# Scattering expert outputs with a bare one-hot selection, split rows, and token weights applied in the residual sum

## The reference

```python
def moe_ffn(h, w_router, w_e_gate, w_e_up, w_e_down):
    logits = jnp.einsum('bsd,de->bse', h, w_router, preferred_element_type=jnp.float32)
    top_vals, top_idx = lax.top_k(logits, TOP_K)          # TOP_K = 2
    top_w = jax.nn.softmax(top_vals, axis=-1)
    combine = jnp.sum(jax.nn.one_hot(top_idx, N_EXPERTS) * top_w[..., None], axis=-2)
    y = jnp.zeros_like(h)
    for e in range(N_EXPERTS):                            # 8 experts, inner width 1408
        y = y + combine[..., e:e + 1] * swiglu(h, w_e_gate[e], w_e_up[e], w_e_down[e])
    return y
...
x = x + moe_ffn(h, w_router[i], w_exp_gate[i], w_exp_up[i], w_exp_down[i])
```

## Time and profile before

| | |
|---|---|
| median of 3 runs | 1165.09 us (1164.87 to 1167.19) |
| profiled execution | 1167.5 us, its span 1165.8 us |
| PE busy | 1100.5 us (94%) |
| PEld busy | 942.7 us (81%) |
| DVE busy | 823.7 us (71%) |
| ACT busy | 669.9 us (57%) |
| expert stage | about 728 us to 1160 us of the span |

### The profile page before, as it was taken

The page is one execution under the profiler, slowest core; times in us unless marked ns, Lnnn a source line. Parts: engine busy times, 40 slices in busy tenths (PEclk is TensorE's granted clock), DMA queues, the critical chain, the costliest instruction groups (busy, mean ns, idle before and its releaser), DMA issues.

```text
span 1165.8 us, 16875 instructions
## 1 busy us (share of the span) xinstructions
PE 1100.5 (94%) x6535; PEld 942.7 (81%) x6535; DVE 823.7 (71%) x1110; ACT 669.9 (57%) x956; POOL 73.9 (6%) x119
## 2 busy tenths in 40 slices
PE   4999999988999998999999996999999999999997
PEld 3979777778999997979787775888888888788885
DVE  3577766875545545457866776689898888989885
ACT  3567655454434435457755553576767676677763
POOL 4001430000000000000521000000000000000000
PEclk9999999998999999999999996799999999999999
DMA  5553354465446444345344454499899898999992
GB/s 180 202 181 118 116 174 145 145 215 202 161 170 239 153 163 151 101 145 181 102 161 144 147 193 166 142 322 339 301 324 365 290 346 307 381 305 349 342 327 90
DMA packets 147670, 250.19 MB, mean 215 GB/s; under 512 B 5166, under 2 KB 108676, under 8 KB 147588
## 3 DMA queue, kind: packets, MB, share of 16 engines
q1 hardware_dynamic: 145808, 246.89, 61.6%
q10 hardware_dynamic: 1780, 2.19, 0.6%
HBM read 248.02 MB, written 1.05 MB: 214 GB/s over the span
## 4 chain that ended last, share of the span: by engine, by line
PE 82%; DVE 10%; ACT 4%; issue 2%; POOL 1%; DMA 1%; ACTq 0%; DVEq 0%; POOLq 0%
PE PS L622 26%; PE PS L1077 9%; PE PS L1078 9%; PE PS L1079 9%; PE PS L938 5%; PE PS L940 5%; PE PS L939 5%; DVE w_lo L402 4%; PE PS L1048 2%; PE PS L710 2%; DVE m_lo L1759 2%; PE PS L648 1%; PE PS L1036 1%; ACT w_hi L393 1%; PE PS L805 1%
## 5 line engine op out<-in xcount | busy, mean ns | idle before, releaser
L402 DVE TENSOR_TENSOR w_lo<-ring,w_hi 128x1536 fp32r<-128x1536 f32 (+1 forms) x192 | 311.6, 1633 | 126.4 <-ACT w_hi L393 125.9
L393 ACT ACTIVATE w_hi<-ring 128x1536 fp32r<-128x1536 f32 (+1 forms) x192 | 264.8, 1388 | 152.5 <-PE PS L940 85.8
L1759 DVE TENSOR_TENSOR m_lo<-ring,m_hi 128x512 fp32r<-128x512 f32 (+2 forms) x256 | 185.7, 754 | 91.9 <-ACT m_hi L1275 90.2
L1275 ACT ACTIVATE m_hi<-ring 128x512 fp32r<-128x512 f32 (+2 forms) x256 | 157.5, 631 | 141.7 <-PE PS L622 139.1
L1077 PE MATMUL PS<-w_hi,hTe 128*96 128x384 f32 (+1 forms) x384 | 131.5, 342 | 0.7 <-issue 0.7
L622 PE MATMUL PS<-m_hi,h_hi 128*128 128x512 f32 (+2 forms) x352 | 125.2, 356 | 2.1 <-DVE m_lo L1759 2.1
L1078 PE MATMUL PS<-w_hi,hTe 128*96 128x384 f32 (+1 forms) x384 | 124.5, 324 | 0.0
L1079 PE MATMUL PS<-w_lo,hTe 128*96 128x384 f32 (+1 forms) x384 | 124.5, 324 | 0.0
L622 PE MATMUL PS<-m_lo,h_hi 128*128 128x512 f32 (+2 forms) x352 | 120.5, 342 | 0.0
L622 PE MATMUL PS<-m_hi,h_lo 128*128 128x512 f32 (+2 forms) x352 | 120.5, 342 | 0.0
L938 PE MATMUL PS<-h_hi,w_hi 128*128 128x256 f32 x352 | 100.6, 286 | 0.8 <-DVE h_lo L1741 0.8
(11 more groups left out here) (320 smaller groups left out, 2197.6 us busy)
## 6 DMA issues: line engine op xcount, KB each, us to landing
ring<-in_w_in_dram SPq DMA_DIRECT2D x40, 1024.0 KB, 5.1
ring<-in_w_exp_gate_dram SPq DMA_DIRECT2D x24, 1536.0 KB, 7.8
ring<-in_w_exp_up_dram SPq DMA_DIRECT2D x24, 1536.0 KB, 9.2
ring<-in_w_exp_down_dram SPq DMA_DIRECT2D x24, 1536.0 KB, 8.5
ring<-in_w_branch_dram SPq DMA_DIRECT2D x12, 1024.0 KB, 4.9
ring<-in_w_ffn_gate_dram SPq DMA_DIRECT2D x6, 1536.0 KB, 6.5
ring<-in_w_ffn_up_dram SPq DMA_DIRECT2D x6, 1536.0 KB, 7.1
ring<-in_w_ffn_down_dram SPq DMA_DIRECT2D x6, 1536.0 KB, 6.4
```

Of the source, the lines that this page charges most:

```text
L393: act.activation(split_parts(u, j)[0], ring[:, i % NSLOT, w0:w0 + words], ACT.Copy)\
L402: dve.tensor_tensor(lo, ring[:, (j // 2) % NSLOT, w0:w0 + words], hi.bitcast(F32), SUB).then_inc(sem(f"lo_ready{b}"), 1)
L1275: act.activation(hi, raw, ACT.Copy).then_inc(sem("m_hi_ready"), 1)
L1759: dve.tensor_tensor(lo, raw, hi.bitcast(F32), SUB).then_inc(sem("m_lo_ready"), 1)
```

## The change

`wsel` goes: the selection that is transposed to `selT` is `psel` itself, ones and zeros. The rows leave PSUM in two parts: ACT writes `ye_hi` for both column halves, and DVE writes `ye_lo` for both, each after ACT's. The scatter becomes two fp32r matmuls into the same bank, one with each part. The token weight of the expert, a value for each partition, multiplies in DVE's add, which becomes a `scalar_tensor_tensor`. Of `weigh`, the reduction for the pass count stays where it was (`most_rows`), because it reads a PSUM bank; the rest moves to between expert 0 and expert 1 on DVE. The new tensors lie over memory that was in use before (`big` and `qk`).

```diff
-        htok_lo, = over(("htok_lo", [P, TT, D], F32R))
+        htok_lo, ye_hi, ye_lo = over(("htok_lo", [P, TT, D], F32R), ("ye_hi", [P, D], F32R), ("ye_lo", [P, D], F32R))
...
             def scatter(r, e, n, part):
-                pe.wait_ge(sem("ye_act"), n + 1)
-                pe.wait_ge(sem("ye_dve"), n + 1)
+                pe.wait_ge(sem("ye_lo_ready"), 2 * n + 2)
                 for c in (2 * part, 2 * part + 1):
                     b, uses = aux_use(r, "scatter", e + 1, c)
                     wait_aux_free(pe, b, uses)
                     a, d = divmod(c, 2)
-                    pe.matmul(PS[:, 4 + b, :], selT[:, e, a * P:(a + 1) * P], ye[:, d * 512:(d + 1) * 512],
-                              start=True, stop=True).then_inc(sem(f"aux_full{b}"), 1)
+                    rows, w = selT[0:CAP, e, a * P:(a + 1) * P], slice(d * 512, (d + 1) * 512)
+                    pe.matmul(PS[:, 4 + b, :], rows, ye_hi[0:CAP, w], start=True, stop=False)
+                    pe.matmul(PS[:, 4 + b, :], rows, ye_lo[0:CAP, w], start=False, stop=True).then_inc(sem(f"aux_full{b}"), 1)
...
             def prepare(r, part):
-                pe.wait_ge(sem("sel_ready"), 2 * (r + 1))
...
-                                              wsel[:, a, 2 * c + i, :], ident[:, :])
+                                              psel[:, a, 2 * c + i, :].bitcast(F32), ident[:, :])
...
             def rows_out(n):                                   # ACT
                 wait_used(act, expert_unit(n), HALVES - 1)
-                act.activation(ye[:, 0:512], PS[0:CAP, 6, :], ACT.Copy).then_inc(sem("ye_act"), 1)
+                for c in range(2):
+                    act.activation(ye_hi[0:CAP, c * 512:(c + 1) * 512], PS[0:CAP, 6 + c, :], ACT.Copy).then_inc(sem("ye_hi_ready"), 1)
...
             def rows_out(n):                                   # DVE
-                wait_used(dve, expert_unit(n), HALVES - 1)
-                dve.tensor_copy(ye[:, 512:1024], PS[0:CAP, 7, :]).then_inc(sem("ye_dve"), 1)
+                for c in range(2):
+                    w = slice(c * 512, (c + 1) * 512)
+                    dve.wait_ge(sem("ye_hi_ready"), 2 * n + c + 1)
+                    dve.tensor_tensor(ye_lo[0:CAP, w], PS[0:CAP, 6 + c, :], ye_hi[0:CAP, w].bitcast(F32), SUB)\
+                       .then_inc(sem("ye_lo_ready"), 1)
...
-                    dve.tensor_tensor(x, x, PS[:, 4 + b, :], ADD).then_inc(sem(f"aux_free{b}"), 1)
+                    dve.scalar_tensor_tensor(x, PS[:, 4 + b, :], wt[:, a, e - 1:e], x, MUL, ADD).then_inc(sem(f"aux_free{b}"), 1)
...
                 if isinstance(r, int):
-                    weigh()
+                    most_rows()
                 dve.wait_ge(sem("psel_ready"), 2 * (r + 1))
-                for a in range(TT):
-                    dve.tensor_tensor(wsel[:, a], psel[:, a].bitcast(F32), wt[:, a, :].unsqueeze(2).broadcast_to([P, NE, CAP]), MUL)\
-                       .then_inc(sem("sel_ready"), 1)
...
                 for e in range(NE):
+                    if e == 1 and isinstance(r, int):
+                        weigh()
                     expert(r, e, n + e)
```

More of the change, by code:

```diff
@@ L260, in hybrid_trunk @@
         y_parts = {0: (yA_hi, yA_lo), 2: (yB_hi, yB_lo), 1: (yA_hi, yA_lo)}
-        psel, = over(("psel", [P, TT, NE, CAP], F32R))
+        psel, _, selT = over(("psel", [P, TT, NE, CAP], F32R), ("qk_mid", [P, 512], F32), ("selT", [P, NE, T], F32R))
         qk = sb("qk", [P, 4096])
@@ L300, in hybrid_trunk @@
         hidf = big[:, 5120:5120 + 3 * T].rearrange("p (f t) -> p f t", f=3)
-        selT = qk[0:CAP, 2048:2048 + NE * T].rearrange("p (e t) -> p e t", e=NE)
-        wsel = big[:, 2048:2048 + TT * NE * CAP].rearrange("p (a e c) -> p a e c", a=TT, e=NE)
-        ye = big[0:CAP, 3584:3584 + D]
         sile = big[0:CAP, 4608:4608 + 2 * GB].rearrange("p (f t) -> p f t", f=2)
@@ L1096, in expert @@
                         if name == "D0" and j % 2 == 0 and not (isinstance(n, int) and n == 0):
-                            pe.wait_ge(sem("ye_act"), n)
-                            pe.wait_ge(sem("ye_dve"), n)
+                            pe.wait_ge(sem("ye_lo_ready"), 2 * n)
                         for x in range(gn):
@@ L1611, in expert @@
                                 wait_aux_full(act, b, uses)
-                                act.activation(selT[:, 2 * c:2 * c + 2, :], two(PS[0:CAP, 4 + b, :]), ACT.Copy)\
+                                act.activation(selT[0:CAP, 2 * c:2 * c + 2, :], two(PS[0:CAP, 4 + b, :]), ACT.Copy)\
                                    .then_inc(sem(f"aux_free{b}"), 1)
@@ L2153, in expert, with most_rows @@
                         rest_lo(dve, expert_unit(n), j)
+            def most_rows():
+                step(dve.tensor_reduce(rsm[:, 8:9], PS[:, 1, TT * NE:(TT + 1) * NE], AX.X, MAX))
             def weigh():
@@ L2164, in weigh @@
                     step(dve.scalar_tensor_tensor(wt[:, a, :], m12[:, a, 0, :], rsm[:, 4 + a:5 + a], wt[:, a, :], MUL, ADD))
-                step(dve.tensor_reduce(rsm[:, 8:9], PS[:, 1, TT * NE:(TT + 1) * NE], AX.X, MAX))
                 step(dve.tensor_scalar(rsm[:, 9:10], rsm[:, 8:9], float(CAP), 1.0, ALU.is_gt, ADD))
```

## The result

The changed kernel took 1159.45 us (median of 6 runs, 1156.50 to 1160.19) against 1167.22 for the kernel before on the same chips (6 runs, 1164.87 to 1167.72): a ratio of 0.9933, 95% interval 0.9922 to 0.9943, or 7.8 us less. Forecast were 10.1 us less, from a median of 1165.09 that three more runs moved up to 1167.22. Single executions that took over 200 us longer than the others are left out of every median and ratio.

What follows compares the result with a forecast made beforehand. PE was taken to bound the expert loop, with DVE close behind. The loop's 8.3 us plus 2.0 in the opening less 0.2 at the end made 10.1, from 1165.09 to 1155.0 us; range 1151.5 to 1159.5.

Steps and rivals of the forecast that it cites:

- opening, to expert 0: Ahead of expert 0: DVE no longer delays PE's second low gather, so PE gains 2.0 us.
- experts 2 to 7: Expert loop: shorter scatter pairs save 1.58 us an expert, less a new 0.28 wait; six experts give 7.8.
- expert 1: Moved `weigh` makes DVE late: PE starts some 0.1 late, the last scatter waits some 1.0, 0.5 us is kept.
- The new wait for the bank: Second scatter pair: PE waits for DVE's add to free the bank, about 0.28 us an expert.
- `hdT_lo`: Before half 8: ready still 0.3 us before PE needs it, no wait, but first place a slower add would show.
- Rival A: Whole kernel: DVE never late, add 0.68 us, waits on banks and `weigh` vanish; 12.9 less, 1152.2 us; chance 0.16.
- the band that the time fell into: Whole kernel: 1157.5 to 1162 us, DVE or loads late by another 0.5 per expert; chance 0.14.
- Rival C: DVE's multiply-add from PSUM is dear, 1.37 us; kernel 5.2 slower, 1170.3 us; chance 0.04.
- Rival D: Scatters on PE save nothing, with 128-column weight loads between; 1165 or a little above; chance 0.06 shared with Rival B.
- the clock: Opening and expert 0: rise moves with the work, 2.0 us gained; staying would give 1.0, coming earlier up to 4.
- Rival B: Expert loop: weight transfers become the bound, the loop gains nothing; 1163.3 us; chance 0.06 shared with Rival D.
- the signs of being wrong: Multiply-adds over 0.9, ACT waiting for the ring, a half 8 wait in every expert, PE still waiting near 730 us.

Runs made afterwards that it cites:

- Experiment 5: Changed kernel with the scatter in one plain fp32 part as before, keeping bare selection, weighted add and moved `weigh`: 1166.31 us, ratio 0.9995 to the kernel before.
- experiment 4: Changed kernel with the second scatter pair and its two DVE adds one half later, after half 5: 1156.67 us, ratio 0.9916 to the kernel before.
- experiment 6: Changed kernel with the low part of the rows left out of the scatter product, though still computed: 1158.63 us, ratio 0.9917 to the kernel before.
- experiment 7: Changed kernel with the token weight left out of DVE's add, a plain tensor_tensor: 1157.42 us, ratio 0.9910 to the kernel before.
- experiment 9: Changed kernel, second scatter pair after half 9 (half 5 in experts 1, 3), `weigh` inside expert 0, scatters awaiting only their own low column half: 1154.89 us.
- experiment 1: Changed kernel with the ten small instructions of `weigh` back in the opening, `wsel` still gone: 1159.26 us, ratio 0.9926 to the kernel before.
- experiment 2: Changed kernel with `weigh` and the two `wsel` multiplications back in the opening, their result unused: 1159.34 us, ratio 0.9934 to the kernel before.

## Why the prediction came out as it did

| term | forecast | measured |
|---|---|---|
| opening, to expert 0 | -2.0 | -1.97 |
| clock in expert 0, and its handover to expert 1 | +0.1 | +1.17 |
| experts 2 to 7 | -7.8 | -7.30 |
| expert 1 | -0.6 | -0.39 |
| end | +0.2 | +0.26 |
| ahead of the first gather | 0 | +0.46 |
| sum | -10.1 | -7.8 |

The spans differ by 7.8. The line ahead of the sum is what one execution happened to get, and says nothing of the change.

**The mechanism was right.** PE bounds the loop, the split rows pay there and pairs take 0.92 to 0.93. Experiment 5 shows it by taking that part away. The new wait for the bank stood where the prediction had put it, and experiments 4, 6, 7 and 9 move it as the reasoning says. `hdT_lo` was the next to be late (experiment 4). Rival A, DVE never late, is out. The reason given with the band that the time fell into, DVE or loads late by another 0.5 us an expert, does not hold either: the experts gave 0.09 less each than forecast, and most of what is missing went to the clock. Rivals C and D are out as well: the adds take 0.74 where 0.75 was taken, and weight loads of 128 columns cost nothing extra beside 512 columns.

**Mis-sized: the clock.** The prediction knew of the choice (2.0 if the rise moves with the work, 1.0 if it stays) and took the wrong one. Where the granted clock steps from its lower to its higher level, in four profiles (us of the span; the earlier rise is one in the first layer):

| | an earlier rise | first gather | expert 0 starts | rise in expert 0 | expert 0 took |
|---|---|---|---|---|---|
| before | 273.94 | 727.54 | 737.76 | 741.57 | 51.12 |
| changed | 274.67 | 728.00 | 736.25 | 742.29 | 52.29 |
| experiment 1 | 273.43 | 727.83 | 736.32 | 741.05 | 51.55 |
| experiment 2 | 274.69 | 728.09 | 738.31 | 742.32 | 51.22 |

The rise comes 467.63 us after the earlier one in all twelve profiles, whether expert 0 began 8.2 or 10.2 us after the first gather. To the first gather its distance is less firm, 13.2 to 14.3 us. So it keeps a time of its own, closing the gap at 730 to 732 us did not bring it earlier, and matmuls that are pulled ahead of it run at 1.2 GHz. Expert 0 pays for that with half of the added time between its start and the rise: 6.04 us against 3.81 in the kernel before, and half of the difference is 1.1. The sentence on the Trainium skill's rule (TensorE: Matmul & The Clock Gate, What's actually happening), that the grid of the gate does not restart with the kernel's work, was the better guide: it gave up to 1 less, and the runs have 1.07 less (1.17 without the 0.1 of expert 1's late start). Whether a larger shift of the work would make the clock rise at another time, no run shows.

**Mis-sized: the bank wait.** 0.28 forecast, 0.37 measured, six times. The adds ended where they were expected, 0.03 and 0.69 us after PE wanted the first bank (forecast 0.02 and 0.68). But the prediction let PE start 0.06 after the second add's end, and the handover takes some 0.15. It counts once the wait is real.

**Mis-sized: expert 1.** It started late by 0.1 as forecast, and took 0.39 less against a forecast of 0.6. The forecast for `weigh` was sound, but the prediction never asked if moving it was worth anything: in the opening it would have cost 0.23 at most (experiment 1), here it costs 0.9. Of the 0.2 that is missing, 0.1 is the same handover as above; the rest was not looked into.

**Rival B half woke.** Loads made no expert longer in the changed kernel's two profiles. In five of the other nine profiles of edited kernels ACT waited for them, 0.9 to 4.6 us in all, one of the signs of being wrong that the prediction had named. At 347 to 351 GB/s against 339 the margin is smaller, and an expert at 49.5 us may be near what the loads allow. No run shows that; one that takes another microsecond off PE without making DVE late would tell.

## What to carry to other kernels

When the pacing engine is relieved, list what frees its buffers and subtract the relief from each margin; the smallest is the new wait, and it includes the handover. An instruction moved out of a critical chain belongs where its engine is idle for longer than it lasts, not merely off the chain. Where the clock rises at a time of its own, as here, work that is pulled ahead of the rise gains only half: 1.97 us were gained in the opening, and 1.07 were paid back in expert 0.

## What the runs showed of the hardware that was not expected

The clock's rise stays put: in the changed kernel 18 matmuls of expert 0 ran wholly at the 1.2 GHz level where the kernel before had 11, although PE's longest idle time between the first gather and expert 0 was shorter (0.70 us against 1.80). At full clock a plain fp32 matmul over 512 columns costs 0.86 us, and the two fp32r ones that replace it 0.46, with the same number of records. The multiply-add on DVE with a scalar for each partition, over 512 PSUM elements, takes 0.740 us, 0.06 more than the plain add. And two executions of one program differed by 3.1 us at the first gather, 2.8 of them from the first 40 us, where their granted clocks differ.
